# Every chunk of the second block's input begins nine columns further into its slot

## The reference

```python
x = first_block(x, c, w_ada, ..., w_in, ..., w_out)    # modulation, two kinds of attention, gates
x = second_block(x, meta_tokens_2, ...)                # below

def second_block(...):                                 # 16 meta tokens ahead of x: 272 rows
    r = concatenate([meta, x])
    h = rmsnorm(r, mix_pre_g)
    mix = mixer_block(h, ...)                          # h @ w_in (2048 x 8200), attention, pooling, gates
    r = r + rmsnorm(mix, mix_post_g)
    h = rmsnorm(r, ffn_pre_g)
    ff = conv_ffn(h, ...)                              # h @ w_up (2048 x 11264), 3-tap conv, gelu, w_down
    return (r + rmsnorm(ff, ffn_post_g))[:, 16:]
```

## Time and profile before

| what | value |
|---|---|
| median of three runs | 2042.51 us |
| the profiled execution | 2043.46 us |
| its span, first to last instruction | 2041.6 us |
| PE busy | 2004.8 us, 98% |
| DVE busy | 1291.7 us, 63% |
| ACT busy | 986.9 us, 48% |
| HBM read | 388.39 MB, 191 GB/s over the span |
| mean granted TensorE clock | 0.994 |

### The profile page before, as it was taken

How to read it: one execution, slowest core, us unless ns; L and a number is a source line. 1 busy time by engine, 2 the same in 40 slices (tenths; PEclk the granted TensorE clock), 3 DMA queues, 4 the chain that set the end, 5 groups by cost and what they waited for, 6 DMA issues and landing times.

```text
span 2041.6 us, 39414 instructions
## 1 busy us (share of the span) xinstructions
PE 2004.8 (98%) x15340; PEld 1911.7 (94%) x15340; DVE 1291.7 (63%) x1670; ACT 986.9 (48%) x1434; POOL 139.4 (7%) x148
## 2 busy tenths in 40 slices
PE   6999999999999999999999999999999999999998
PEld 5989999999999999999999999999999999988886
DVE  6686778775677544444457754766776676665545
ACT  3244455555645544444445454644444445444444
POOL 0000000000002000000004210000100000000000
PEclk9899999999999999999999999999999999999999
DMA  9897866565545666555544555366566555655554
GB/s 350 313 330 236 284 209 214 177 203 165 160 165 166 175 176 175 172 148 145 153 144 156 191 195 160 116 204 186 164 184 197 186 173 181 212 199 189 194 188 143
DMA packets 188103, 391.75 MB, mean 192 GB/s; under 512 B 11955, under 2 KB 17632, under 8 KB 185568
## 3 DMA queue, kind: packets, MB, share of 16 engines
q1 hardware_dynamic: 186992, 388.03, 59.5%
q10 hardware_dynamic: 1024, 2.51, 0.4%
HBM read 388.39 MB, written 2.10 MB: 191 GB/s over the span
## 4 chain that ended last, share of the span: by engine, by line
PE 92%; DMA 3%; DVE 3%; ACT 1%; SPq 1%; issue 0%; DVEq 0%; ACTq 0%
PE acc L838 21%; PE acc L839 20%; PE acc L840 20%; DMA ada_w<-in_w_ada 2%; PE psum_y L839 2%; PE psum_x L839 2%; PE psum_x L840 2%; PE psum_x L838 2%; PE psum_y L840 2%; PE psum_y L838 2%; PE acc L1267 2%; PE acc L1269 2%; PE acc L1268 2%; DMA raw<-in_w_in 1%; DVE w_lo L1865 1%; PE psum_x L1267 1%
## 5 line engine op out<-in xcount | busy, mean ns | idle before, releaser
L1865 DVE TENSOR_TENSOR w_lo<-raw,w_hi 128x1024 fp32r<-128x1024 f32 (+1 forms) x644 | 810.7, 1272 | 618.0 <-ACT w_hi L1331 615.5
L1331 ACT ACTIVATE w_hi<-raw 128x1024 fp32r<-128x1024 f32 (+1 forms) x644 | 671.6, 1050 | 802.3 <-PE acc L840 520.7
L838 PE MATMUL acc<-act_hi,w_lo 128*128 128x258 f32 (+2 forms) x3424 | 977.0, 285 | 9.7 <-DVE w_lo L1865 5.7
L839 PE MATMUL acc<-act_lo,w_hi 128*128 128x258 f32 (+2 forms) x3424 | 965.3, 282 | 0.0
L840 PE MATMUL acc<-act_hi,w_hi 128*128 128x258 f32 (+2 forms) x3424 | 965.0, 282 | 0.0
L838 PEld LDWEIGHTS acc<-act_hi,w_lo 128*128 128x128 f32 x3424 | 647.0, 189 | 19.6 <-issue 10.5
L839 PEld LDWEIGHTS acc<-act_lo,w_hi 128*128 128x128 f32 x3424 | 647.6, 189 | 0.6 <-issue 0.5
L840 PEld LDWEIGHTS acc<-act_hi,w_hi 128*128 128x128 f32 x3424 | 647.2, 189 | 0.0
L838 PE MATMUL psum_x<-act_hi,w_lo 128*128 128x258 f32 x352 | 99.5, 283 | 0.0
L839 PE MATMUL psum_y<-act_lo,w_hi 128*128 128x258 f32 x352 | 99.3, 282 | 0.0
L840 PE MATMUL psum_y<-act_hi,w_hi 128*128 128x258 f32 x352 | 99.3, 282 | 0.0
(11 more groups left out here) (328 smaller groups left out, 2280.0 us busy)
## 6 DMA issues: line engine op xcount, KB each, us to landing
raw<-in_w_in SPq DMA_DIRECT2D x272, 512.0 KB, 3.7
raw<-in_w_ffn_up SPq DMA_DIRECT2D x176, 512.0 KB, 4.4
raw<-in_w_ffn_down SPq DMA_DIRECT2D x88, 512.0 KB, 4.4
ada_w<-in_w_ada SPq DMA_DIRECT2D x64, 512.0 KB, 10.4
raw<-in_w_out SPq DMA_DIRECT2D x64, 512.0 KB, 4.0
ada_x<-in_w_ada SPq DMA_DIRECT2D x16, 1024.0 KB, 5.9
raw<-in_w_attn_o SPq DMA_DIRECT2D x16, 512.0 KB, 3.8
raw<-in_w_pool_o SPq DMA_DIRECT2D x16, 512.0 KB, 4.4
```

What stands on the lines that cost most here:

```text
L838: pe.matmul(out, w_lo, a_hi, start=c == 0, stop=False)
L839: pe.matmul(out, w_hi, a_lo, start=False, stop=False)
L1331: act.activation(M.hi[s][:, 0:job.width], M.raw[s][:, 0:job.width], ACT.Copy).then_inc(M.hi_ready[s], 1)
L1865: dve.tensor_tensor(M.lo[s][:, 0:job.width], M.raw[s][:, 0:job.width], M.hi[s][:, 0:job.width].bitcast(FP32), ALU.subtract).then_inc(M.lo_ ...
```

## The change

A constant INTO = 9 is added to the column at which a chunk of `act2_hi` and `act2_lo` begins, wherever one of the two is addressed: PE's reads, ACT's writes, and DVE's reads and writes. The slots, their pitch and the arrays' places stay.

```diff
 PITCH = 320
+INTO = 9
@@ memory
     def act2(k, c0, n):
-        return M.act2_hi[:, PITCH * k + c0:PITCH * k + c0 + n], M.act2_lo[:, PITCH * k + c0:PITCH * k + c0 + n]
+        return M.act2_hi[:, INTO + PITCH * k + c0:INTO + PITCH * k + c0 + n], M.act2_lo[:, INTO + PITCH * k + c0:INTO + PITCH * k + c0 + n]
@@ act_program
     def hi2_of(k, n):
-        return M.act2_hi[:, PITCH * k + ROWS - n:PITCH * k + ROWS]
+        return M.act2_hi[:, INTO + PITCH * k + ROWS - n:INTO + PITCH * k + ROWS]
@@ dve_program
-    part2_hi = lambda k, n: M.act2_hi[:, PITCH * k + ROWS - n:PITCH * k + ROWS].bitcast(FP32)
-    part2_lo = lambda k, n: M.act2_lo[:, PITCH * k + ROWS - n:PITCH * k + ROWS]
+    part2_hi = lambda k, n: M.act2_hi[:, INTO + PITCH * k + ROWS - n:INTO + PITCH * k + ROWS].bitcast(FP32)
+    part2_lo = lambda k, n: M.act2_lo[:, INTO + PITCH * k + ROWS - n:INTO + PITCH * k + ROWS]
```

## The result

The changed kernel takes 2024.85 us (median of six, 2018.98 to 2027.20); the kernel before, run beside it, 2040.71 (2037.92 to 2046.81). The ratio is 0.9905, with a 95% interval of 0.9887 to 0.9923: faster by 0.95%. Forecast were 2050 us and slower; the time also lies outside the range of 2026 to 2072. The profiled execution took 2024.87 us, with a span of 2023.1.

What follows compares the result with a forecast made beforehand. PE was taken as the bound, at its start-to-start spacing per product. Terms of +7.0 and +0.5 us summed to +7.5, giving 2050.0 us by the median (own ends 2044 to 2061); the range was 2026 to 2072.

Steps and rivals of the forecast that it cites:

- PE is the bound, its spacing is the price, and nothing else is touched: Whole kernel: PE busy 98% of the span, so each nanosecond per product reaches the end undiminished; no instruction or wait differs.
- DVE's and ACT's 128 operations: 64 roundings on ACT and 64 remainders on DVE write the moved columns; their extra cost was taken as 0.
- 6960 products at +1.0 ns: 258-column products of g2, pool_w, pool_o, out2 and up get slower: +7.0 us, from +4.2 to +16.0.
- 1584 products at +0.3: 272-column products of qkv2, f2 and u2 get 0.3 ns slower each: +0.5 us, from -2.7 to +2.2.
- The weights' start as a partner: TensorE's spacing surplus depends on how moving-operand reads and next-weight reads fall on each other; a step is 4.2 ns.
- rival 2: Second block's 258-column products: the new start is better, kernel faster; 2013 us, or 2033 in a third of them; chance 0.22.
- The 4.2 ns: Step between two steady spacings of 256-column products in the first block, 117.6 and 113.4 ns, applied to 258-column products.
- 156 takes them past it: 258-column reads began 8 bytes before the weights' place (120 against 128); the new start lies beyond it.
- The argument against it: Every attn_o group with a remainder start of 128 or more is slower than 119.0 ns.
- Rival 1: Moved reads on TensorE: the address doesn't matter, only panel noise is left; 2042.5 us within 3; chance 0.27.
- rival 3: Moved products: odd word starts break reads, 4.8 ns each; 2084 us, 2056 at a third, middle 2070; chance 0.11.
- The line rule: Moved reads touch one more 16-byte SBUF line, 66 for 65 or 69 for 68; equal shares would give +15.6 us.

Runs made afterwards that it cites:

- e2: Changed kernel with offsets per job (qkv2 10, pool_o 8, out2 6, up 7) in place of 9 everywhere; 2054.41 us.
- e6: Changed kernel, but out2 and up move only the rounded array, pool_o, g2 and qkv2 only the remainder; 2037.60 us.
- The map: Spacings by d, bytes from weight-read to moving-read start, gathered over the runs; four runs for it changed only job offsets: 2050.91, 2041.00, 2033.45, 2054.40 us.
- e7: Changed kernel with every weight slot and every moving operand 64 bytes further; 2025.57 us.
- e8: Changed kernel with weight slots and the second block's chunks 32 bytes further, first block's chunks unmoved; 2038.46 us.
- e4: Changed kernel with the weight slots 64 bytes further, moving operands where they were; 2070.71 us.
- e10: The first map run's kernel with 64 instead of 128 stationary columns in six second-block jobs, leaving out half their output features; 2037.36 us.
- e5: Changed kernel with offset 9 only in pool_w, pool_o, out2 and up, 0 in qkv2, f2, u2 and g2; 2024.95 us, ratio 0.9893.

## Why the prediction was wrong

- *PE is the bound, its spacing is the price, and nothing else is touched*: right. Of the profiled executions' 18.5 us, 16.7 are found in the jobs whose input moved; the other 1.8 are in the first block, which the change doesn't touch, so this part of the gain is chance. That DVE's and ACT's 128 operations cost nothing: right (4 ns at most on one).
- *6960 products at +1.0 ns*: this is the step that failed. Measured are -3.5 ns, outside the term's ends of +0.6 and +2.3. The neighbours in attn_o (starts 152 and 160) had been read at 120.4 and 119.6; as steady streams they are 118.7 and 120.0 (e2). So the rows priced the neighbours within 1.7 ns, though in attn_o the rounded and the remainder operand stand at different distances, and e6 shows that such mixed products don't cost the mean of their single prices. The main error was to go from the neighbours to 156 by a mean. The map has no slope between starts four bytes apart, so a neighbour binds nothing, and the ends should have been those of the single steps, wide on both sides.
- *1584 products at +0.3*: the sign is right, the size is 3.3, over the upper end of 1.4 a product. The ends came from 258-column groups, whose spread of 1.7 is under the 6.7 ns that the 272-column map covers (123.3 to 130.0).
- *The weights' start as a partner*: the prediction held that for rival 2, at 0.22. That the partner matters is what happened: e7 and e8 show that the distance decides, e4 that the weights' side alone can move a spacing, e10 that half the weight read takes most of the spread away. Its price and its direction were luck. The 4.2 ns came from out_b and qk_a, two spacings at one and the same distance, which is another effect than the 3.5 ns between two distances. And "156 takes them past it" is no reason: past the weights' start, +12 costs 123.3 and +64 122.2. The argument against it, that all groups of attn_o at 128 or more were above 119.0, had weighed eight of 64 places as if they were all.
- *Rival 1* is refuted by the map (115.6 to 123.3 ns for the same products), *rival 3* by the after kernel itself (odd starts at 115.6) and by up in e2 (an odd start at 120.0, where 4.8 more had been priced). The line rule of the Trainium skill ("SBUF — State Buffer", section "Specifications (TRN2)"), as the prediction worked it out, would have had every odd start dearer by a line; this case's +28 and +44 have that line more than d = -8's 119.1 and cost 115.6 and 115.7, so it isn't what sets this spacing.
- The Trainium skill, "TensorE: Matmul & The Clock Gate", section "Step-by-step: what each phase is for", gives PE two independent read ports, one for the moving operand and one for the weights. Here the two reads are not independent in time: out_b's unmoved moving read costs 6.7 ns more when the weights' start moves (e4), and pool_o 7.7 ns less when half as much is loaded and written (e10).

## What to carry to other kernels

Where PE's stream sets the time, take the spacing from start to start and divide by the columns; if it is several ns above them, the distance between the starts of the moving and the weight reads may be worth 1% of a kernel, in either direction, for no instruction. In this kernel it couldn't be reasoned out from neighbours. Give each stage its own offset in one run and read all spacings from one trace, check one address in more than one stage, since it can have two spacings, and when arrays are added ahead of others keep that distance (e4, the changed kernel with one base address 64 bytes on, took 2070.71 us against its 2024.85).

## What the runs showed of the hardware that was not expected

- One address can have two steady spacings. The changes were seen at borders of pieces and panels, and a state is kept in between: v_a at 113.3 in its first panel and 117.8 in its second before the change; qkv2 of e5 at 123.3 and then 126.7; out2 and up of e4 at 116.7 and 120.0; down 228.9 in eleven kernels and 233.3 in six. Unchanged code falls on either side: qk_a's first 288 products took 117.7 each before the change and 113.4 after, which is 1.2 of the first block's 1.8 us. Down's states alone are 1008 x 4.4 ns = 4.4 us, about half of the 8 us between the slowest and the fastest execution of one kernel. That these states are the cause of that spread is argued, not shown.
- Many of the steady spacings, at a granted clock of 1.00, are whole multiples of 8 periods of 2.4 GHz: 113.3 ns is 272 of them, 116.7 280, 120.0 288, 123.3 296, 126.7 304, 130.0 312, 233.3 560. Some are so only as means: up in e4 alternates between 117 and 123 ns, qkv2 after the change between 129 and 124. Others (115.6, 119.1, 228.9 and most of the map's between them) are no such multiple; 115.6 is the mean of steps of 116, 114 and 117 ns that repeat.
